# A hybrid backbone in one program: the held expert tile as 64 tokens by two slots, summed by TensorE alone

## The chip, the cores and the metric

One core of a Trainium2 chip runs the whole program once. The metric is the device time in microseconds (us), as the median of several executions. Engines: PE is TensorE, DVE VectorE, ACT ScalarE, POOL GpSimd, SP the engine that issues most plain transfers.

## What is computed

Two layers over 512 latent and 256 context tokens of width 1024. A layer is a modulated RMS norm, one input projection whose columns feed a gated delta rule, a Fourier branch and a convolution branch, an output projection, and then PEER, a retrieval of single-neuron experts. PEER is what the change touches:

```python
def blk(args):                 # 128 tokens; 128 experts for each of them
    hb, eb, gb = args
    act = jax.nn.gelu(jnp.einsum("tkd,td->tk", u_tab[eb], hb))
    return jnp.einsum("tk,tkd->td", gb * act, v_tab[eb])
```

For each token, 128 rows of 8 KB (a U row and a V row of 1024 floats) are gathered; each U row gives a dot product with the token's vector h, its gelu times the gate weight gives a coefficient, and the V rows are summed with these coefficients. The sum goes into the residual stream through a gate.

## The kernel before

All is f32. A tile is 128 tokens, a slot is the k-th of the 128 experts of every token of a tile. One slot is one indirect DMA from POOL that gathers 128 rows of 8 KB (1.05 MB), one dot product on DVE (L347, L2606), three small steps on ACT (gelu, gate weight, and the coefficients on the diagonal of a 128x128 matrix), and two matmuls on PE, diagonal by V row half, that add into two PSUM banks.

The function peer does the tiles of layer 0, six of them, but leaves out the last one (context tokens 128 to 255). That held tile is done by class HeldTile inside projection_latents, the stage in which layer 1's input projection of the latent tokens is computed, so that gathers run beside matmuls. The stage in order:

- SP loads four pieces of h (L759), three of 18 weight chunks, waits for the last row's store, and goes on with the chunks as PE uses them up (L766).
- PE does 18 chunks of 8 matmuls of 512 columns (L779); after k = 0, 2, 3, 5, 6, 7 it calls held.pe for one slot. In chunks 7 to 14 an 8-column matmul (L791) sums squares. Then come four row blocks, of 8 times two matmuls of 264 columns (L801, L803), with five slots each. PE does its queue in order: a slot whose diagonal isn't ready stops the products behind it.
- ACT calls held.act for six slots a chunk, then copies the chunk's product out of PSUM (L820), and from chunk 6 on does a silu (L824) and to chunk 13 a square (L830) of an earlier chunk. Silu and gelu need different tables (ACT_TABLE_LOAD). In a row block it does five slots and three copies (L855 to L857).
- DVE does the dots, and between them the taps of the two convolutions.
- POOL gathers into a ring of six buffers (HELD_RING); before gather g it waits until slot g - 6 is used up.

The held tile's slots are shared between two engines. on_dve says which: in chunks 6 to 17 every third slot, elsewhere two of three. A slot on DVE is added by one scalar_tensor_tensor (L369) to yacc, one on PE by diagonal (L386) and two matmuls (L397) to PSUM banks 1 and 3. That gives 67 slots to PE and 61 to DVE. The next stage, branches_beside_context, adds the two sums (L1101).

The first six gathers of the held tile are issued at the end of peer, on POOL, behind the last tile's gathers and a wait for the tile's expert numbers (eid_ready). In peer, SP's queue is a loop over the tiles; its last turn (i = M) waits for x_ready, which DVE signals when the last tile's sum is in the residual, and stores the row (L2556). A stage ends with a barrier of all engines behind the last instruction of each.

## Time and profile before

| | us |
|---|---|
| median of 3 runs (4364.39 to 4365.87) | 4364.73 |
| the profiled execution, whole | 4367.23 |
| its span | 4365.4 |
| PE busy in the span | 3693.1 |
| DVE busy | 3006.0 |
| ACT busy | 1720.2 |
| POOL busy | 1645.7 |
| the held stage, start to start of the next | 2310.6 to 2690.6 |

"Busy" is the time in which an engine executes something; PE's ends are modelled, so start-to-start times are the safer reading for it. PEclk is the clock that TensorE was granted, as a share of full speed. The DMA share is the mean busy share of 16 DMA engines. In brackets behind a timeline row stands the idle time before it and what ended it. "x4" on a PE row is four instructions; an f32 matmul is two of them. A shape such as 128*64 is rows by columns of the weights.

### The profile page before, as it was taken

What the parts mean: (1) busy time and instruction counts of PE and PEld (TensorE: products, weight loads), DVE (VectorE), ACT (ScalarE), POOL (GpSimd) and SP (SyncE); (2) the same over time, 40 slices, a digit from 0 to 9 for tenths busy, and PEclk for the clock granted to TensorE, in tenths of its full rate; (3) what the DMA queues carried; (4) which work ended last, traced back from release to release, by engine and by line L of the source; (5) the groups of instructions that cost most, each with busy time, mean ns of one, the idle gap of its engine ahead of it and who ended that gap; (6) DMA issues with size and microseconds to landing.
All of it is one profiled execution on the core that took longest, in us unless ns stands there. A gap on an engine that the chain in (4) does not pass through costs nothing. (4 is left out here: it accounts for less than half of the span.)

```text
span 4365.4 us, 55131 instructions
## 1 busy us (share of the span) xinstructions
PE 3693.1 (85%) x18945; PEld 1903.6 (44%) x18945; DVE 3006.0 (69%) x6251; ACT 1720.2 (39%) x5270; POOL 1645.7 (38%) x1508
## 2 busy tenths in 40 slices
PE   7998998988888887888886888888898888888777
PEld 3566854533433433433432335775443343343222
DVE  3964666975775875875875885557797687687444
ACT  2223623444344344344342454353444433433333
POOL 0004513443443443444443432352444444444332
PEclk9999999999999999999998999899999999999999
DMA  8360159999999999999999997015999999999997
GB/s 336 122 239 29 37 198 367 416 421 421 418 415 422 414 417 421 407 420 422 410 412 369 408 394 303 2 37 190 404 422 421 421 421 421 421 413 421 422 421 325
DMA packets 238985, 1506.07 MB, mean 345 GB/s; under 512 B 28433, under 2 KB 33617, under 8 KB 71153
## 3 DMA queue, kind: packets, MB, share of 16 engines
q0 software_dynamic: 184320, 1342.26, 74.7%
q1 hardware_dynamic: 54384, 160.28, 9.9%
q8 instruction: 150, 2.46, 0.2%
q14 instruction: 131, 1.07, 0.1%
HBM read 1490.32 MB, written 12.12 MB: 344 GB/s over the span
## 5 line engine op out<-in xcount | busy, mean ns | idle before, releaser
L2831 PE MATMUL ps<-low,pediag 128*128 128x512 f32 x2180 | 1058.7, 615 | 226.1 <-ACT pediag L2741 219.3
L2606 DVE CUSTOM_DVE_ANT_0 low<-low,hc 128x1024 f32<-128x1024 f32 x545 | 667.8, 1225 | 359.3 <-DMA low<-in_experts_dram,eid 342.0
L2585 POOL DMA_INDIRECT low<-in_experts_dram,eid x539 | 595.0, 1104 | 812.4 <-PE ps L2831 783.2
L2733 ACT ACTIVATE low<-peact 128x1 f32<-128x1 f32 x1152 | 232.1, 201 | 1335.0 <-DVE peact L2606 1334.0
L2831 PEld LDWEIGHTS ps<-low,pediag 128*128 128x128 f32 x2180 | 388.9, 192 | 824.5 <-ACT pediag L2741 499.4
L2741 ACT ACTIVATE pediag<-cst,low 128x128 f32<-128x128 f32 x1152 | 462.5, 402 | 42.1 <-PE ps L2831 4.5
L2831 PE MATMUL ps<-wide_a,pediag 128*128 128x512 f32 x640 | 307.8, 612 | 54.4 <-ACT pediag L2741 54.2
L2736 ACT ACTIVATE low<-low,gw 128x1 f32<-128x1 f32 x1152 | 339.1, 294 | 37.4
L2831 PE MATMUL ps<-wide_b,pediag 128*128 128x512 f32 x640 | 303.3, 605 | 50.7 <-ACT pediag L2741 48.5
L2060 PEld LDWEIGHTS ps<-qkvT,arena 128*128 128x128 f32 x2560 | 312.0, 193 | 75.4 <-issue 75.4
L2060 PE MATMUL ps<-qkvT,arena 128*128 128x128 f32 x2560 | 313.1, 276 | 2.4 <-ACT qkvT L2024 2.4
L2606 DVE CUSTOM_DVE_ANT_0 wide_a<-wide_a,hc 128x1024 f32<-128x1024 f32 x160 | 196.2, 1226 | 97.3 <-DMA wide_a<-in_experts_dram,eid 91.2
L2606 DVE CUSTOM_DVE_ANT_0 wide_b<-wide_b,hc 128x1024 f32<-128x1024 f32 x160 | 196.2, 1226 | 96.9 <-DMA wide_b<-in_experts_dram,eid 91.4
L2585 POOL DMA_INDIRECT wide_a<-in_experts_dram,eid x158 | 169.8, 1074 | 237.4 <-PE ps L2831 232.7
L2831 PE MATMUL ps<-last_b,pediag 128*128 128x512 f32 x456 | 219.4, 608 | 46.2 <-ACT pediag L2741 44.9
L2831 PE MATMUL ps<-last_a,pediag 128*128 128x512 f32 x456 | 220.5, 612 | 43.0 <-ACT pediag L2741 41.6
L2585 POOL DMA_INDIRECT wide_b<-in_experts_dram,eid x158 | 176.2, 1115 | 195.8 <-PE ps L2831 188.5
L2831 PEld LDWEIGHTS ps<-wide_a,pediag 128*128 128x128 f32 x640 | 114.4, 193 | 227.1 <-ACT pediag L2741 134.8
L2831 PEld LDWEIGHTS ps<-wide_b,pediag 128*128 128x128 f32 x640 | 113.5, 189 | 217.5 <-ACT pediag L2741 120.5
L2606 DVE CUSTOM_DVE_ANT_0 low<-last_b,hc 128x1024 f32<-128x1024 f32 x114 | 139.7, 1225 | 80.9 <-DMA last_b<-in_experts_dram,eid 77.6
L2606 DVE CUSTOM_DVE_ANT_0 low<-last_a,hc 128x1024 f32<-128x1024 f32 x114 | 139.6, 1225 | 76.1 <-DMA last_a<-in_experts_dram,eid 72.2
L2585 POOL DMA_INDIRECT last_b<-in_experts_dram,eid x112 | 121.4, 1084 | 163.1 <-PE ps L2831 156.0
(497 smaller groups left out, 5773.9 us busy)
## 6 DMA issues: line engine op xcount, KB each, us to landing
pjdot<-in_mod_t_dram SPq DMA_DIRECT2D x64, 512.0 KB, 5.2
arena<-in_w_mod_dram SPq DMA_DIRECT2D x24, 1024.0 KB, 14.4
arena<-in_peer_wq_dram SPq DMA_DIRECT2D x8, 2048.0 KB, 17.1
low<-in_experts_dram,eid POOLq DMA_INDIRECT x609, 8.7
pjw<-in_w_cols_dram SPq DMA_DIRECT2D x18, 512.0 KB, 3.7
plw<-in_w_cols_dram SPq DMA_DIRECT2D x18, 512.0 KB, 8.1
x_rows<-low SPq DMA_DIRECT2D x10, 512.0 KB, 7.7
qkvT<-mod_rows SPq DMA_DIRECT2D x9, 512.0 KB, 7.6
```

The costliest lines, as they stand in the source:

```text
L2060: last = self.nc.tensor.matmul(self.kit.ps[:, 4 + q % 2, 0:P], self.kit.wq[:, i, q * P:(q + 1) * P], self.hT[:, i, :], start=i == 0, stop= ...
L2585: nc.gpsimd.indirect_dma_start(ring.row(g), None, table, bass.IndirectOffsetOnAxis(eid[:, j % 2, k:k + 1], 0)).then_inc(ring.landed(g), 16)
L2606: nc.vector.tensor_tensor_reduce(out=dot_out if final else ring.row(g)[:, 0:D], in0=ring.row(g)[:, 0:D], in1=hc[:, j % 2, :], scale=1.0, s ...
L2733: nc.scalar.activation(ge[:, g % 2, 0:1], act_v[:, j % 2, k:k + 1], ACT.Gelu_apprx_tanh).then_inc(gelu_ready, 1)
L2736: nc.scalar.activation(ge[:, g % 2, 1:2], ge[:, g % 2, 0:1], ACT.Copy, scale=gw[:, j % 2, k:k + 1]).then_inc(weighed, 1)
L2741: nc.scalar.activation(diag[:, g % DIAGS, :], ident, ACT.Copy, scale=ge[:, g % 2, 1:2]).then_inc(diag_ready, 1)
L2831: last = nc.tensor.matmul(ps[:, half, :], diag[:, g % DIAGS, :], ring.row(g)[:, D + half * 512:D + (half + 1) * 512], start=k == 0, stop=k ...
```

## The change

What it does:

- The held tile is laid out anew: gather g brings 64 tokens' rows for two slots (partitions 0 to 63 the one, 64 to 127 the other); gathers 0 to 63 are for tokens 0 to 63, the others for tokens 64 to 127. For this the expert numbers, the gate weights and h are copied between partitions by small DMAs (spread, spread_rows).
- All 128 slots are summed on PE: the weights are a 128x64 matrix, two diagonals one above the other, so a matmul sums the two slots. The V row's left half goes to PSUM partitions 0 to 63, the right half to 64 to 127. A ring of four such matrices replaces three of 128x128. The adds on DVE and yacc go.
- The next stage gates the four quarters out of PSUM; two of them are moved to their partitions first, by two copies and two matmuls.
- The h pieces and the first three weight chunks are loaded by peer's SP code, behind its loop, into room that the query weights leave. The expert numbers' copies stand between the two. POOL waits for them (eid_in) ahead of the first held gather.
- A matrix of ones leaves the constants.

```diff
+HELD_DIAGS = 4
 HELD_A_CHUNK = 6
 HELD_A_ROW = 5
-HELD_SEMS = ["dotted", "gelu_ready", "weighed", "diag_ready", "summed", "added", "row_saved"]
+HELD_SEMS = ["dotted", "gelu_ready", "weighed", "diag_ready", "summed", "row_saved", "h_in", "w_in", "eid_in", "gw_in",
+             "rows_in"]
...
-        TAPS_FROM, TAPS_TO = 6 * HELD_A_CHUNK, 18 * HELD_A_CHUNK
-        spare = lambda g: g % 3 == 1 if TAPS_FROM <= g < TAPS_TO else g % 3 != 0
-        self.on_dve = [spare(g) for g in range(SLOTS)]
-        self.n_dve = [sum(self.on_dve[:g]) for g in range(SLOTS + 1)]
-        self.n_pe = [g - self.n_dve[g] for g in range(SLOTS + 1)]
-        self.issued = self.dots = self.adds = self.scaled = self.sums = 0
-
-    def work_in(self, parts, yacc):
-
-        self.yacc = yacc
-        self.act_v, self.ge, self.coef = (parts[:, i * SLOTS:(i + 1) * SLOTS] for i in range(3))
-        self.diag = parts[:, 3 * SLOTS:(3 + HELD_DIAGS) * SLOTS].rearrange("p (a n) -> p a n", n=P)
-
-    def free(self, eng, g):
-
-        if self.on_dve[g]:
-            eng.wait_ge(self.added, self.n_dve[g + 1])
-        else:
-            eng.wait_ge(self.summed, self.n_pe[g + 1])
+        self.issued = self.dots = self.scaled = self.sums = 0
+
+    def work_in(self, parts):
+
+        self.act_v, self.ge, self.coef, self.gw = (parts[:, i * SLOTS:(i + 1) * SLOTS] for i in range(4))
+        self.diag = parts[:, 4 * SLOTS:4 * SLOTS + HELD_DIAGS * 64].rearrange("p (a n) -> p a n", n=64)
+
+    def spread(self, sp, out, src, sem):
+
+        for half in range(2):
+            for part in range(2):
+                sp.dma_start(out[part * 64:(part + 1) * 64, half * 64:(half + 1) * 64],
+                             src[half * 64:(half + 1) * 64, part * 64:(part + 1) * 64]).then_inc(sem, 16)
+
+    def spread_rows(self, sp):
+
+        h = self.kit.hc
+        for part in range(2):
+            sp.dma_start(h[part * 64:(part + 1) * 64, 0, :], h[0:64, 1, :]).then_inc(self.rows_in, 16)
+        sp.wait_ge(self.rows_in, 32)
+        sp.dma_start(h[0:64, 1, :], h[64:128, 1, :]).then_inc(self.rows_in, 16)
 
     def gathers(self, pool, upto):
 
         for g in range(self.issued, min(upto, SLOTS)):
             if g >= HELD_RING:
-                self.free(pool, g - HELD_RING)
+                pool.wait_ge(self.summed, g - HELD_RING + 1)
             self.gather(g)
...
-            bass.IndirectOffsetOnAxis(self.eid[:, g:g + 1], 0)).then_inc(self.e_in[g % HELD_RING], 16)
+            bass.IndirectOffsetOnAxis(self.kit.eid2[:, g:g + 1], 0)).then_inc(self.e_in[g % HELD_RING], 16)
...
     def dve(self, dve, n):
 
         for g in range(self.dots, self.dots + n):
+            if g % 64 == 0:
+                dve.wait_ge(self.rows_in, 32 + 16 * (g // 64))
             row = self.rows[g % HELD_RING][:, 0:D]
             dve.wait_ge(self.e_in[g % HELD_RING], 16 * (g // HELD_RING + 1))
-            self.nc.vector.tensor_tensor_reduce(out=row, in0=row, in1=self.h, scale=1.0, scalar=0.0, op0=ALU.mult,
-                                                op1=ALU.add, accum_out=self.act_v[:, g:g + 1]).then_inc(self.dotted, 1)
-            if g >= 2:
-                self.add(dve, g - 2)
+            self.nc.vector.tensor_tensor_reduce(out=row, in0=row, in1=self.kit.hc[:, g // 64, :], scale=1.0, scalar=0.0,
+                                                op0=ALU.mult, op1=ALU.add, accum_out=self.act_v[:, g:g + 1]
+                                                ).then_inc(self.dotted, 1)
         self.dots += n
...
-    def add(self, dve, g):
-
-        if not self.on_dve[g] or g < self.adds:
-            return
-        self.adds = g + 1
-        row, coef = self.rows[g % HELD_RING][:, D:2 * D], self.coef[:, g:g + 1]
-        dve.wait_ge(self.weighed, g + 1)
-        if self.n_dve[g] == 0:
-            self.nc.vector.tensor_scalar(self.yacc, row, coef, None, ALU.mult).then_inc(self.added, 1)
-        else:
-            dve.wait_ge(self.added, self.n_dve[g])
-            self.nc.vector.scalar_tensor_tensor(out=self.yacc, in0=row, scalar=coef, in1=self.yacc,
-                                                op0=ALU.mult, op1=ALU.add).then_inc(self.added, 1)
-
...
     def act(self, act, n):
 
         for g in range(self.scaled, self.scaled + n):
+            if g == 0:
+                act.wait_ge(self.gw_in, 64)
             act.wait_ge(self.dotted, g + 1)
             self.nc.scalar.activation(self.ge[:, g:g + 1], self.act_v[:, g:g + 1], ACT.Gelu_apprx_tanh
                                       ).then_inc(self.gelu_ready, 1)
             act.wait_ge(self.gelu_ready, g + 1)
             self.nc.scalar.activation(self.coef[:, g:g + 1], self.ge[:, g:g + 1], ACT.Copy,
                                       scale=self.gw[:, g:g + 1]).then_inc(self.weighed, 1)
-            if not self.on_dve[g]:
-                i = self.n_pe[g]
-                act.wait_ge(self.weighed, g + 1)
-                if i >= HELD_DIAGS:
-                    act.wait_ge(self.summed, i - HELD_DIAGS + 1)
-                self.nc.scalar.activation(self.diag[:, i % HELD_DIAGS, :], self.kit.c("ident"), ACT.Copy,
-                                          scale=self.coef[:, g:g + 1]).then_inc(self.diag_ready, 1)
+            act.wait_ge(self.weighed, g + 1)
+            if g >= HELD_DIAGS:
+                act.wait_ge(self.summed, g - HELD_DIAGS + 1)
+            self.nc.scalar.activation(self.diag[:, g % HELD_DIAGS, :], self.kit.packed("I")[:, 0, :], ACT.Copy,
+                                      scale=self.coef[:, g:g + 1]).then_inc(self.diag_ready, 1)
         self.scaled += n
 
     def pe(self, pe, n):
 
         for g in range(self.sums, self.sums + n):
-            if not self.on_dve[g]:
-                i = self.n_pe[g]
-                pe.wait_ge(self.diag_ready, i + 1)
-                for half, b in enumerate(self.BANKS):
-                    last = self.nc.tensor.matmul(self.kit.ps[:, b, :], self.diag[:, i % HELD_DIAGS, :],
-                                                 self.rows[g % HELD_RING][:, D + half * 512:D + (half + 1) * 512],
-                                                 start=i == 0, stop=i == self.n_pe[SLOTS] - 1)
-                last.then_inc(self.summed, 1)
+            pe.wait_ge(self.diag_ready, g + 1)
+            for half in range(2):
+                last = self.nc.tensor.matmul(self.kit.ps[half * 64:(half + 1) * 64, self.BANKS[g // 64], :],
+                                             self.diag[:, g % HELD_DIAGS, :],
+                                             self.rows[g % HELD_RING][:, D + half * 512:D + (half + 1) * 512],
+                                             start=g % 64 == 0, stop=g % 64 == 63)
+            last.then_inc(self.summed, 1)
         self.sums += n
...
-                for t in range(NL):
-                    sp.dma_start(hT[:, :, t * P:(t + 1) * P], h_d[t].rearrange("p (k n) -> p k n", k=KD)
-                                 ).then_inc(h_in, 16)
+                held.spread_rows(sp)
+                held.spread(sp, held.gw, kit.gw[:, held.j % 2, :], held.gw_in)
+                sp.wait_ge(held.row_saved, 16)
                 for c, off in enumerate(chunks):
-                    if c == RING:
-                        sp.wait_ge(held.row_saved, 16)
-                    if c >= RING:
+                    if c < RING:
+                        continue
+                    if c >= 2 * RING:
                         sp.wait_ge(proj_ready, c - RING + 1)
                     sp.dma_start(w[:, c % RING, :, :], w_chunk(kit, L, off)).then_inc(w_in[c % RING], 16)
...
-                pe.wait_ge(h_in, 16 * NL)
+                pe.wait_ge(held.h_in, 16 * NL)
+                pe.wait_ge(held.w_in, 16 * RING)
                 for c in range(NF):
-                    pe.wait_ge(w_in[c % RING], 16 * (c // RING + 1))
+                    w_now = w[:, c % RING] if c >= RING else held.w[:, c]
+                    if c >= RING:
+                        pe.wait_ge(w_in[c % RING], 16 * (c // RING))
                     if c >= 2:
                         pe.wait_ge(proj_read, c - 1)
...
+                pe.wait_ge(far_read, 2)
+                for at, rows in ((lo, hi), (hi, lo)):
+                    last = nc.tensor.matmul(ps[at, 7, :], ident[:, rows], far[:], start=True, stop=True)
+                last.then_inc(far_moved, 1)
...
-                for c in range(2):
-                    last = nc.vector.tensor_tensor(two(moved)[:, c, :], two(yacc)[:, c, :], ps[:, 1 + 2 * c, :], ALU.add)
-                link(last)
+                nc.vector.tensor_copy(far[hi, :], ps[hi, 1, :]).then_inc(far_read, 1)
+                nc.vector.tensor_copy(far[lo, :], ps[lo, 3, :]).then_inc(far_read, 1)
                 for c in range(2):
                     dve.wait_ge(mean_ready, c + 1)
                     nc.vector.tensor_tensor(acc[:, c, :], acc[:, c, :], ps[:, 2 * c, :], ALU.subtract
                                             ).then_inc(cent_ready, 1)
                 dve.wait_ge(gate_in, 16)
-                link(nc.vector.tensor_tensor(moved, moved, gate_c, ALU.mult))
+                left, right = slice(0, 512), slice(512, D)
+                for rows, cols, bank in ((lo, left, 1), (hi, right, 3), (lo, right, 7), (hi, left, 7)):
+                    if bank == 7:
+                        dve.wait_ge(far_moved, 1)
+                    last = nc.vector.tensor_tensor(moved[rows, cols], ps[rows, bank, :], gate_c[rows, cols], ALU.mult)
+                link(last)
...
                 sp.wait_ge(x_saved, 16 * (M - 1 if held else M))
+                if held:
+                    sp.wait_ge(sc.q_ready, HP * (N - 1) + LATE)
+                    for t in range(NT - NC):
+                        sp.dma_start(held.hT[:, :, t * P:(t + 1) * P], kit.h_d[t].rearrange("p (k n) -> p k n", k=KD)
+                                     ).then_inc(held.h_in, 16)
+                    sp.wait_ge(sc.eid_ready, late_numbers + N - 1)
+                    held.spread(sp, kit.eid2, eid[:, (N - 1) % 2, :], held.eid_in)
+                    for c in range(PL_RING):
+                        sp.dma_start(held.w[:, c], w_chunk(kit, L + 1, latent_chunks()[c])).then_inc(held.w_in, 16)
...
                 if held:
-                    pool.wait_ge(sc.eid_ready, late_numbers + N - 1)
+                    pool.wait_ge(held.eid_in, 64)
                     pool.wait_ge(sc.q_ready, HP * (N - 1) + LATE)
```

## Rows read from the trace of the kernel before

**Rows 1.** Windows: us, busy of PE, PEld, DVE, ACT, POOL, PEclk, DMA share, GB/s

```profile
2328.80:2461.00 132.20, 101.25 (x203) 40.83 (x201) 94.73 (x129) 40.48 (x117) 57.97 (x46) 0.92 0.97 391
...
2461.00:2633.00 172.00, 153.48 (x337) 61.40 (x338) 150.77 (x221) 86.76 (x209) 64.96 (x60) 0.98 0.99 393
...
2633.00:2690.60 57.60, 48.06 (x168) 32.17 (x166) 41.12 (x55) 29.97 (x72) 20.87 (x16) 0.94 0.85 325
```

**Rows 2.** Timeline (start us, us, engine): ScalarE's copies of chunks 0, 7, 12, 17

```profile
2339.22 0.60 ACT L820 ACTIVATE arena<-ps 128x512 f32<-128x512 f32 x1 [18.48 <-PE ps L779]
...
2461.01 0.58 ACT L820 ACTIVATE arena<-ps 128x512 f32<-128x512 f32 x1
...
2547.96 0.60 ACT L820 ACTIVATE arena<-ps 128x512 f32<-128x512 f32 x1 [0.84 <-PE ps L779]
...
2632.98 0.60 ACT L820 ACTIVATE arena<-ps 128x512 f32<-128x512 f32 x1 [3.56 <-PE ps L779]
```

**Rows 3.** Timeline, ScalarE's path from chunk 11's copy to the next slot on PE

```profile
2530.91 0.60 ACT L820 ACTIVATE arena<-ps 128x512 f32<-128x512 f32 x1 [1.16 <-PE ps L779]
...
2534.13 1.28 ACT L376 ACT_TABLE_LOAD   x1
...
2535.98 0.40 ACT L386 ACTIVATE parts<-cst,parts 128x128 f32<-128x128 f32 x1
...
2536.44 1.98 PE L397 MATMUL ps<-arena,parts 128*128 128x512 f32 x4 [1.90 <-ACT parts L386]
```

**Rows 4.** Timeline of PE: products, a slot, an 8-column sum, a product

```profile
2511.88 1.88 PE L779 MATMUL ps<-wide_a,plw 128*128 128x512 f32 x4
2513.59 1.88 PE L397 MATMUL ps<-low,parts 128*128 128x512 f32 x4
2515.40 1.02 PE L791 MATMUL ps<-arena 128*8 128x512 f32 x2
2516.36 1.12 PE L779 MATMUL ps<-wide_a,plw 128*128 128x512 f32 x2
```

**Rows 5.** Timeline of PE in the scan: 64-column weights, alternate halves, 128 columns

```profile
2953.96 1.09 PE L1846 MATMUL ps<-scS,arena 128*64 128x128 f32 x16
2954.88 1.04 PE L1855 MATMUL ps<-scS,qkvT 128*64 128x128 f32 x16
```

**Rows 6.** Timeline at the change from the last tile to the held stage

```profile
2302.51 0.94 POOL L333 DMA_INDIRECT low<-in_experts_dram,eid  x1 [0.30 <-issue]
...
2309.47 0.32 SPq L2556 DMA_DIRECT2D x_rows<-qkvT  x1
...
2310.84 9.32 SPq L759 DMA_DIRECT2D wide_a<-h_turned  x4
...
2326.94 2.04 PE L779 MATMUL ps<-wide_a,plw 128*128 128x512 f32 x2 [20.02 <-DMA plw<-in_w_cols_dram]
...
2328.78 2.68 PE L397 MATMUL ps<-arena,parts 128*128 128x512 f32 x4
```

**Rows 7.** Waits in the held stage: total us, times, longest

```profile
POOL low L333 <- DVE low L369: 67.4, 33, 4.7
```

**Rows 8.** Timeline of ScalarE in the row blocks and at their end

```profile
2650.61 0.39 ACT L855 ACTIVATE low<-ps 128x264 f32<-128x264 f32 x1 [4.09 <-PE ps L803]
...
2652.65 0.20 ACT L376 ACTIVATE parts<-parts 128x1 f32<-128x1 f32 x1
...
2688.77 0.39 ACT L855 ACTIVATE low<-ps 128x264 f32<-128x264 f32 x1 [0.32 <-PE ps L803]
```

**Rows 9.** DMA issues of whole span, then both stage changes: median landing last

```profile
pjw<-in_w_cols_dram SPq DMA_DIRECT2D x18, 512.0 KB, 3.7
...
wide_a<-h_turned SPq DMA_DIRECT2D x4, 512.0 KB, 8.3
...
cialog<-in_a_log_dram SPq DMA_DIRECT2D x1, 4.0 KB, 10.4
```

**Rows 10.** Timeline of VectorE in the stage after

```profile
2707.24 1.23 DVE L1112 SCALAR_TENSOR_TENSOR arena<-arena 128x1024 f32<-128x1024 f32 x1 [7.95 <-DMA arena<-mod_rows]
```

More of the change, by code:

```diff
@@ L35 @@
 NEG = -3.0e38
-CONSTS = (["ident", "L0", "L1", "M0", "M1", "CH0", "CH1", "ones", "gmean", "C64", "S64"]
+CONSTS = (["ident", "L0", "L1", "M0", "M1", "CH0", "CH1", "gmean", "C64", "S64"]
           )
@@ L717, in _, with latent_chunks, projection_latents @@
                 nc.gpsimd.memset(row_eps[0:H, :], EPS * P).then_inc(padded, 1)
-def projection_latents(nc, kit, L, h_d, hT, qkvT, zs, ab, fT, acc, held):
+def latent_chunks():
+    return ([C_OFF + c * P for c in range(4)] + [c * P for c in range(NQKV)] + [F_OFF + c * P for c in range(2)])
+def projection_latents(nc, kit, L, room, qkvT, zs, ab, fT, acc, held):
     NCV, NFN = 4, 2
-    chunks = ([C_OFF + c * P for c in range(NCV)] + [c * P for c in range(NQKV)]
-              + [F_OFF + c * P for c in range(NFN)])
+    chunks = latent_chunks()
     ROWS = SEQ // GRID_W
     W = GRID_W + 2 * HALO
-    RING = 3
+    RING = PL_RING
     NF = len(chunks)
@@ L744, in projection_latents @@
         ZH = ZA // 2
-        two = lambda at: kit.arena[:, at:at + 2 * SEQ].rearrange("p (c n) -> p c n", c=2)
+        hT = held.hT
+        two = lambda i: room[:, i * 2 * SEQ:(i + 1) * 2 * SEQ].rearrange("p (c n) -> p c n", c=2)
         wz = kit.arena[:, 0:KD * ZA].rearrange("p (k n) -> p k n", k=KD)
-        at = KD * ZA
-        aT, gT, pT, yT = (two(at + i * 2 * SEQ) for i in range(4))
-        sq, root = aT, kit.arena[:, at + 2 * SEQ:at + 3 * SEQ]
+        aT, gT, pT, yT = (two(i) for i in range(4))
+        sq, root = aT, room[:, 2 * SEQ:3 * SEQ]
         at = PL_SPREAD
@@ L778, in _ @@
                     for k in range(KD):
-                        last = nc.tensor.matmul(ps[:, b, :], w[:, c % RING, k, :], hT[:, k, :],
+                        last = nc.tensor.matmul(ps[:, b, :], w_now[:, k, :], hT[:, k, :],
                                                 start=k == 0, stop=k == KD - 1)
@@ L910, in _ @@
                 held.dve(dve, NL * HELD_A_ROW)
-                held.settle(dve)
                 dve.wait_ge(root_turned, 1)
@@ L992, in branches_beside_context @@
         csq = sb("csq", [P, 2, SEQ])
+        far = sb("far", [P, 512])
+        lo, hi = slice(0, 64), slice(64, P)
         hT = sb("hT", [P, KD, CTX])
@@ L2979, in constants @@
          "M1": same & (i < j), "CH0": (i < CHUNK) & (j >= 0), "CH1": (i >= CHUNK) & (j >= 0),
-         "ones": np.ones((P, P)), "gmean": (i // 64 == j // 64) / 64.0}
+         "gmean": (i // 64 == j // 64) / 64.0}
     ang = 2 * np.pi * ((i % 64) * (j % 64) % 64) / 64
```

37 lines of the change are left out of this document (18 added, 19 removed).

## The prediction

> **What bounds the kernel now.** I read the windows of the held stage first: what each engine and the DMA did in its three parts [rows 1]. The stage runs from 2310.6 to 2690.6 us. In the middle part, 2461 to 2633, the DMA share reads 0.99 at 393 GB/s, which looks like a DMA bound, while PE is busy for 153.5 of 172 us and VectorE for 150.8. So the shares don't settle it, and I went to the order of events. ScalarE's copies of the chunks' products (L820) mark the 18 chunks [rows 2]: chunk 0 at 2339.22, chunk 7 at 2461.01, chunk 12 at 2547.96, chunk 17 at 2632.98. From chunk 11 [rows 3] to chunk 12 it is 17.05 us, and six of the ten steps from chunk 7 on are 17.04 to 17.06. So even a period is that of a fixed chain, not of transfers.
>
> The chain is readable in one chunk [rows 3]. The last product of chunk 11 lets ScalarE copy at 2530.91; it then loads a table, does a silu and a square, loads the table back (2534.13) and builds the next slot's diagonal, which ends at 2536.38; PE, 1.90 us idle, starts that slot at 2536.44. From copy to slot is 5.53 us, and nothing of it is the slots' cost. A chunk then has 7 more product matmuls and, on PE, slots. A 512-column f32 matmul is two MATMUL instructions: four take 2513.59 - 2511.88 = 1.71 us [rows 4], so an instruction is 0.43, a matmul 0.855, a slot's pair 1.71. In the period stand 7 x 0.855 = 5.98 and three of the four PE slots of these chunks (the fourth follows the last product and lies beside ScalarE's path): 5.98 + 3 x 1.71 + 5.53 = 16.64, and 0.4 for the way from the last product to the copy and for changes of mode gives the 17.05. PE and ScalarE in turn set this part. VectorE and GpSimd aren't on it, though GpSimd waits long for VectorE's adds [rows 7]: the next gathers already stand behind it, and DVE isn't what PE waits for.
>
> **The change, part by part.** The profiled execution took 4367.23 us (span 4365.4), the median is 4364.73; I add differences in us to the profiled one and carry the sum to the median, 2.5 lower.
>
> *VectorE's adds go.* The 61 adds of the code leave. In the period above they lie beside PE, so I cost that at nothing from chunk 7 on. The seven steps before that take 121.8 us [rows 2], 17.4 each, with VectorE's padding and first convolutions at their end. I take 16.2 for six of them (PE's own time is 6.84 + 6 x 1.48 = 15.7, see below) and 19 for the last, 116 in all: -5.8. The bounds are 0 (nothing was due to the adds) and -9 (15.7 for the six).
>
> *Every slot goes to PE.* Per chunk six slots instead of two (chunks 0 to 5) or four, per row block five instead of one or two. All depends on what one slot, two calls with 64 columns of weights each, costs between full matmuls; call it S. No row has such a pair with 512 columns between full ones. The nearest is the scan, which writes alternate halves of the partitions with 64-column weights, in the same order of calls: 16 instructions of 128 columns take 2954.88 - 2953.96 = 0.92 us [rows 5]. By the rate of [rows 4], 0.107 for 128 columns, they would take 1.71 in a row. So the two halves do overlap, 2.15 units of time for four instructions. The calls come as A1 A2 B1 B2. Taken in order, A2 must wait for A1 (same columns), B1 starts beside A2, B2 beside the next A1. In a stream this gives 2 units a pair, as seen. A lone pair between full matmuls has nothing beside A1 and B2: 3 units, 1.28. Between full and narrow there is a price: slot to the 8-column sum 1.81 where 1.71 is the work, and that sum to the next full matmul 0.96 where 0.86 is: 0.10 at each change [rows 4]. So S = 1.28 + 0.19 = 1.48. Bounds: 0.86 (full overlap, no change price) and 1.90 (none, with it).
>
> The Trainium skill's "TensorE: Matmul & The Clock Gate", section "Part 3: Packing small matmuls", says that matmuls in distinct column groups run concurrently with starts about 4 ns apart, and "TensorEngine Tiling (Array Packing)", section "Key Properties", that a change of tiling mode drains the array. The trace agrees with both where it can: 0.92 for 1.71, and 0.10 a change. By the first alone a lone pair would be 2 units; rival 1 below works this out from the rows. The same section says that matmuls start and end in program order, and this gives my 3 units, since the halves of one f32 call come first.
>
> Now the sums. Chunk 0: from slot 0 to the copy, 5.98 + 5 S + 0.2 = 13.6, before 10.4 (2328.78 to 2339.22): +3.1. From chunk 7 on the period is 5.98 + 5 S + 5.95 = 19.3 (the 5.95 is 17.05 less the 5.98 and 5.13 above, so it carries all that I can't itemize). The square, 0.65, is missing from the last three: 7 x 19.3 + 3 x 18.65 = 191.1, before 171.97: +19.1. Row blocks: ScalarE copies the first at 2650.61, the last at 2688.77 [rows 8]. After a copy the first gelu is 2.04 us off [rows 8], the first diagonal by three steps of some 0.3 to 0.4 later 3.5; six of the eight steps of two 264-column matmuls, 264/512 of 1.71 = 0.88 each, and four slots stand in the cycle: 3.5 + 4 S + 6 x 0.88 = 14.7, thrice, and 1 for the turned roots (an estimate), 45.2 against 38.2: +7.0. From chunk 17 to the first, 17.6 now, with three more slots of which the longer ScalarE path hides most: +1.5. Together 3.1 - 5.8 + 19.1 + 1.5 + 7.0 = +24.9. The slope is 71 slots, so 71 us for each us of S.
>
> *The first loads, and the way into the stage.* The diff puts them behind SP's loop. SP's queue there first waits for the last row's x_ready, so they can't start before the store at 2309.47 [rows 6]: they are ahead of the stage's start by 1.4 us only. In that queue come four h loads (now issued 2310.84 to 2320.16, 9.3 us), then the four pieces of the expert numbers, then three weight loads. Behind the numbers' semaphore stands GpSimd with the held tile's first six gathers, the last of which it issues at 2302.51 now; and behind GpSimd the barrier that ends the phase, so all engines. Count: h issued 2309.9 to 2317 (less traffic beside them), the numbers land behind them at about 2323 (h landings 8.3 us in the median [rows 9]), six gathers at 0.94 + 0.30 end at 2331, the barrier as now 1.1: the stage starts at about 2332 and not at 2310.6. In it SP must first copy h to both halves and then the gates' weights: two copies, wait, one copy, four small ones. A loaded queue lands a 4 KB load only after 10.4 us [rows 9], the shortest landing on the page is 3.7 us, for 512 KB [rows 9]. The queue empties meanwhile, so I take 4 for the copies and 5 for the small ones, 2 for issuing: 11, then three ScalarE steps 1.0. PE has k 0 of chunk 0 behind it and waits in order for slot 0, at about 2344 by this count. Now it is at 2328.78, after 20.02 us of waiting for weights, which go. So +15 (bounds +8 with short landings, +22 with loaded ones). The stretch from 2302 to 2323 has no gather in the DMA queues; since PE and ScalarE set the later pace, only the start is lost.
>
> *After the stage.* The far halves cost two copies, two narrow matmuls and four quarter products in place of two adds and one product, some +2 us on VectorE, to be ready by 2698. The next thing VectorE waits for lands at 2707.24, after 7.95 us of idleness [rows 10]: nothing. If that cover were gone it would be +2. The smaller constants (no "ones") cost nothing.
>
> **Sum:** +15 + 24.9 = +39.9: profiled 4407.1, median **4405**.
>
> **Rivals.**
> 1. *Full overlap.* A and B run side by side in a lone pair too: 2 units, S = 0.86 + 0.19 = 1.05. For it: the scan's stream doesn't tell 2 units from 3 for a lone pair. Against: A2 stands before B1 in the queue. -0.43 x 71 = -30.4: +9.5, 4374.
> 2. *No overlap, S = 1.90* (512 columns from two places of SBUF are more than the scan's 128). Against: the scan's four are from two places too. +0.42 x 71 = +30, and chunks 1 to 7 become bound by PE (6.84 + 6 x 1.9 = 18.2 each, +14): +84, 4449.
> 3. *Not slower: the pairs are free of the change.* Full overlap and no price for changing the mode, S = 0.86, so 71 x 0.62 = -44, with the short start of +8: 8 + 24.9 - 44 = -11, 4354. It decides from S = 0.91 at a start of +15, or 1.01 at +8; above that it isn't faster. For it: VectorE's 61 adds are truly gone, and GpSimd waits 67.4 us for adds of one tile alone [rows 7]. Against: the 0.10 at each change.
> 4. *The start isn't delayed* (the numbers land early, the barrier overlaps): 0 instead of +15, 4390. Against: SP's order. This is also the case that the change does what its words say, loads a tile ahead; in the diff they aren't.
>
> **How the numbers follow.** Forecast 0.55, rival 1 0.17, rival 2 0.07, rival 3 0.11, rival 4 0.10. A measurement of this kernel can tell about 0.2%, 8.7 us, so 4356 to 4373.5 is no change. Rival 3 gives faster 0.09 and same 0.02; rival 1, at the edge, same 0.09 and slower 0.08; the rest slower: 0.09, 0.11, 0.80. The range leaves out rival 3 and most of rival 2: from rival 1's 4373 to 4428, which is the forecast with the long start and S = 1.7.
>
> **What would show it.** In the profile after: GpSimd's first L333-like gather after 2320 instead of at 2288.6; the stage's first memset at about 2332; slot 0 on PE at 2342 to 2350; a period between chunk copies of 19.3 in place of 17.05, PE idle for some 2 us once in it, and DMA share in the middle down from 0.99 to about 0.88; a lone pair at 1.28 from start to start of its neighbours less 0.2. Wrong it would be if the period stays at 17 (rival 1, then all of the loss is the start), if it is 21.4 (rival 2), or if six gathers are issued before the last row's store.

## The result

The changed kernel takes 4394.6 us (median; 4391.3 to 4398.0), the kernel before 4365.3 in the same job: a ratio of 1.0058, 95% interval 1.0046 to 1.0071, so 29 us slower. The forecast was 4405, "slower". Its direction holds and its size is 10 us too large; below, the terms turn out to be off in both directions. Three slow executions of the runs below (14001 us of e7_order_act, 8453 and 6166 us of e10_h_late_both) are left out of their ratios.

The profiled execution took 4397.01 us, span 4395.0 against 4365.4. First the windows of the kernel after; columns are us, then the busy time of PE, PEld, DVE, ACT, POOL, then PEclk, DMA share, GB/s:

```profile
2300.00:2310.00 10.00, 6.61 (x14) 2.03 (x12) 4.45 (x8) 2.69 (x9) 0.00 (x0) 1.00 0.03 11
2310.00:2324.00 14.00, 0.00 (x0) 0.00 (x0) 0.57 (x1) 0.00 (x0) 1.36 (x2) 0.55 0.95 269
...
2349.20:2475.60 126.40, 113.26 (x314) 29.73 (x314) 64.90 (x104) 51.37 (x157) 55.04 (x47) 0.99 0.99 404
2475.60:2659.70 184.10, 158.89 (x418) 40.60 (x420) 128.92 (x204) 90.20 (x228) 67.52 (x60) 0.94 0.96 370
2659.70:2721.00 61.30, 56.33 (x220) 28.28 (x220) 22.47 (x37) 33.37 (x85) 18.53 (x16) 0.97 0.78 293
```

Against [rows 1], chunks 7 to 17 (second line from below) grew from 172 to 184 us, at fewer GB/s and at a lower PEclk. And from 2300 to 2310 us the DMA engines move next to nothing, where in the kernel before they are full:

```profile
2300.00:2310.00 10.00, 5.92 (x12) 2.00 (x12) 4.91 (x6) 1.79 (x6) 1.97 (x2) 0.99 1.01 421
```

ScalarE's copies of the products of chunks 0, 7 and 17 are the marks, as in [rows 2] (timeline: start us, us, engine):

```profile
2362.85 0.60 ACT L812 ACTIVATE wide_a<-ps 128x512 f32<-128x512 f32 x1 [7.69 <-PE ps L771]
...
2475.59 0.58 ACT L812 ACTIVATE wide_a<-ps 128x512 f32<-128x512 f32 x1
...
2659.71 0.60 ACT L812 ACTIVATE arena<-ps 128x512 f32<-128x512 f32 x1 [6.39 <-PE ps L771]
```

The row blocks' first copy is at 2678.33 and the last at 2719.03 (2650.61 and 2688.77 before, [rows 8]). The last row store of the tile before is 1.1 later than in [rows 6], slot 0 stands at 2349.24. So the sum can be made term by term:

| term, us | forecast | measured |
|---|---|---|
| row store to slot 0 | +15 | 38.64 - 19.31 = +19.3 |
| slot 0 to copy 0 | +3.1 | 13.61 - 10.44 = +3.2 |
| copy 0 to copy 7 | -5.8 | 112.7 - 121.8 = -9.1 |
| copy 7 to copy 17 | +19.1 | 184.1 - 172.0 = +12.2 |
| copy 17 to first row | +1.5 | 18.6 - 17.6 = +1.0 |
| rows | +7.0 | 40.7 - 38.2 = +2.5 |
| sum | +39.9 | +29.1 |

With the tile before (+1.1) that is 30.2 at the last row copy; the spans differ by 29.6.

**The start** in the kernel after, timeline:

```profile
2310.60 0.32 SPq L2559 DMA_DIRECT2D x_rows<-qkvT  x1
2311.03 4.85 SPq L2580 DMA_DIRECT2D arena<-h_turned  x4
2315.92 3.49 SPq L317 DMA_DIRECT2D eid<-eid  x4
2319.45 1.53 SPq L2585 DMA_DIRECT2D arena<-in_w_cols_dram  x3
2322.34 0.94 POOL L337 DMA_INDIRECT arena<-in_experts_dram,eid  x1 [32.89 <-DMA eid<-eid]
...
2325.28 1.17 SPq L324 DMA_DIRECT2D hc<-hc  x2
...
2328.55 0.94 POOL L337 DMA_INDIRECT low<-in_experts_dram,eid  x1 [0.30 <-issue]
2329.49 1.37 POOL L908 MEMSET arena<- 128x1504 f32 x1
...
2337.84 1.23 DVE L353 CUSTOM_DVE_ANT_0 arena<-arena,hc 128x1024 f32<-128x1024 f32 x1 [27.27 <-DMA hc<-hc]
2338.33 2.52 SPq L317 DMA_DIRECT2D parts<-gw  x4
...
2348.28 0.20 ACT L364 ACTIVATE parts<-parts 128x1 f32<-128x1 f32 x1 [42.27 <-DMA parts<-gw]
...
2349.24 1.12 PE L381 MATMUL ps<-arena,parts 128*64 128x512 f32 x2 [20.65 <-ACT parts L372]
```

Read it as a chain: store, expert numbers, first gather (2322.34; 2288.6 before), h copied to both halves (issued 2325.28, landed 2337.84), gate weights (issued from 2338.33, landed 2348.28), slot 0. The engines enter the stage while GpSimd still issues the six gathers (SP's copy at 2325.28, the last gather at 2328.55): the barrier did not stand behind them, as the forecast had it.

**A lone slot** between products, and PE over a short stretch just behind the slot's start:

```profile
2539.82 0.59 PE L771 MATMUL ps<-arena,plw 128*128 128x512 f32 x1
2540.34 1.08 PE L381 MATMUL ps<-low,parts 128*64 128x512 f32 x4
2541.35 1.13 PE L771 MATMUL ps<-arena,plw 128*128 128x512 f32 x2
2542.40 1.08 PE L381 MATMUL ps<-low,parts 128*64 128x512 f32 x4
```

```profile
2540.34 0.65 PE L381 MATMUL ps<-low,parts 128*64 128x512 f32 x2
```

The second view is of 2540.42 to 2540.46 only: two of the slot's four instructions have begun, though one unit of 0.43 isn't over yet; the other two follow half a microsecond behind the first two. The two column halves run side by side, so the work is two units of 0.43. From the slot to the product behind it is 1.01 where 0.86 is the work, from that product to the next slot 1.05 where 0.855 is the product: 0.15 and 0.19 more, 0.35 for both changes together. S = 0.86 + 0.35 = 1.21, between the forecast's 1.48 and rival 1's 1.05.

**A chunk in the stretch from 7 to 17**: the windows of chunks 9 and 10, then PE at the start of chunk 10:

```profile
2494.90:2512.60 17.70, 15.14 (x44) 3.84 (x44) 14.15 (x24) 9.17 (x23) 6.49 (x7) 1.00 0.99 385
2512.60:2531.90 19.30, 16.75 (x44) 4.19 (x44) 13.95 (x23) 9.17 (x23) 6.56 (x7) 0.91 0.93 359
```

```profile
2514.41 1.12 PE L771 MATMUL ps<-arena,plw 128*128 128x512 f32 x2
2518.09 1.08 PE L381 MATMUL ps<-arena,parts 128*64 128x512 f32 x4 [2.55 <-ACT parts L372]
2519.09 3.35 PE L771 MATMUL ps<-arena,plw 128*128 128x512 f32 x4
```

PE's wait for ScalarE at each chunk's start, 1.90 us in [rows 3], is 2.55 now. After it, in five of the ten chunks, the clock falls to its lower level, 1.2 GHz, for a moment: four instructions take 3.35 us where they else take 1.98, and PEclk of the chunk reads 0.91. Three such chunks take 19.3 us against 17.7 of a clean one. The last two of the ten have no square and would take 17.0, as the one before them does:

```profile
2604.30:2621.30 17.00, 15.11 (x44) 3.81 (x44) 12.42 (x20) 8.64 (x22) 8.50 (x7) 1.00 0.97 387
2621.30:2641.20 19.90, 17.05 (x42) 4.41 (x44) 11.52 (x20) 8.65 (x23) 7.60 (x7) 0.83 0.89 328
2641.20:2659.70 18.50, 15.71 (x42) 4.17 (x44) 8.63 (x14) 8.55 (x22) 6.03 (x7) 0.91 0.96 340
```

How many chunks are met is partly chance: with the same wait of 2.55, two of the ten read a lower clock in e1_early below, five in e2_early_all and four in e6_order.

### The profile page after: what moved, and what is told of

Its sections match the earlier page's. It is cut to its first block and busy times, and to the rows that moved or that the text cites. A ratio compares the mean times of both kernels' runs of the same rounds, so it can differ in the third digit from the quotient of the medians.

```text
span 4395.0 us, 55644 instructions
## 1 busy us (share of the span) xinstructions
PE 3713.8 (84%) x19193; PEld 1864.7 (42%) x19193; DVE 2937.1 (67%) x6193; ACT 1735.2 (39%) x5331; POOL 1646.6 (37%) x1508
## 5 line engine op out<-in xcount | busy, mean ns | idle before, releaser
L2843 PEld LDWEIGHTS ps<-wide_b,pediag 128*128 128x128 f32 x640 | 113.5, 189 | 220.9 <-ACT pediag L2753 127.3
L2597 POOL DMA_INDIRECT last_b<-in_experts_dram,eid x112 | 124.1, 1108 | 160.2 <-PE ps L2843 153.1
```

The costliest lines, as they stand in the source:

```text
L2597: nc.gpsimd.indirect_dma_start(ring.row(g), None, table, bass.IndirectOffsetOnAxis(eid[:, j % 2, k:k + 1], 0)).then_inc(ring.landed(g), 16)
L2843: last = nc.tensor.matmul(ps[:, half, :], diag[:, g % DIAGS, :], ring.row(g)[:, D + half * 512:D + (half + 1) * 512], start=k == 0, stop=k ...
```

## The experiments

The theory after reading the two traces: (1) the lost start is SP's chain of small copies; (2) a slot's halves overlap, and S is set by them and the price of the mode change; (3) from chunk 7 on PE and ScalarE in turn set the time, and the longer wait with its clock drops is what was lost. The rivals: the bytes that the DMA engines must move set the start, and the pace as well. Twelve kernels were run; ratios are to the kernel before in the same job.

### Nothing side by side: e3_same_half

```diff
-                last = matmul(ps[half * 64:(half + 1) * 64, BANKS[g // 64], :], ..., start=g % 64 == 0, stop=g % 64 == 63)
+                last = matmul(ps[0:64, BANKS[g // 64], :], ..., start=g % 64 == 0 and half == 0,
+                              stop=g % 64 == 63 and half == 1)
```

> The kernel after, with both products of a slot on the same column half of the array (left and right halves of the V rows are summed in one place, so the part of the output that the held tile gives is not what the reference asks). Nothing can then lie side by side. Theory (the halves run in pairs, A1 with B1 and A2 with B2): a slot's pair takes four units of 0.43 in place of two, so its cost goes from 1.21 to about 2.06 us and the period of a chunk with six slots from 17.7 by 4 x 0.85 for the lone slots and 0.85 or so for the two adjacent ones to 22; over 18 chunks and 4 rows some 75 us more than after, unless the weight loads hide better: 4450 to 4475 us. Rival (no overlap of halves in the kernel after): 4395, the same.

One execution: 4475.2 us, span 4473.1, 78 more than after. A slot and its successor on PE:

```profile
2533.81 1.93 PE L381 MATMUL ps<-low,parts 128*64 128x512 f32 x4
2535.68 1.12 PE L772 MATMUL ps<-arena,plw 128*128 128x512 f32 x2
```

From slot to product it is 1.87 in place of 1.01, two units more, and the period of chunks 7 to 17 is 21.9. By 71 slots the 0.86 would be 61, but with S = 2.07 chunks 0 to 7 are bound by PE as well (137.4 us between copies 0 and 7), as rival 2 had it. So the halves overlap fully, even in a lone slot.

### The loads really a tile ahead: e1_early, e2_early_all, e6_order

```diff
                 for i in range(M + 1):
+                    if held and i == M:
+                        sp.wait_ge(sc.q_ready, HP * (N - 1) + LATE)
+                        ... the four h loads, the respread of eid, the three weight loads
                     if i >= 1:
                         sp.wait_ge(x_ready, i)
```

> The kernel after, with one edit: the first loads of the stage and the respread of the expert numbers are queued on SP before it waits for the last tile's rows, not behind their store; the gate weights and rows of h are still copied in the stage. Theory (the lost start is a chain of waits on SP): the six held gathers leave at about 2290 us and land before the stage starts, slot 0 then waits for the copies of h and of the gate weights alone, landed some 10 + 10 us after the stage's start at about 2312, so slot 0 stands near 2333 where it stood at 2349.2: 16 us less, about 4379 us. Rival (the DMA engines' bytes set the start): 2298 to 2310 us, in which the engines moved next to nothing, hold about 4 MB, so at most 10 us come back, about 4385. Rival (the start is not what costs): 4394.

Measured: 1.0033 (1.0020 to 1.0045), 4384.5 us. By the ratios it is 11 us less than after, but the two intervals nearly touch, so the time alone can't tell the bytes rival's 10 from the 16. Slot 0 stands at 2341.15, 8 us earlier than in the kernel after and not 16.

e2_early_all adds the copies of h (tokens 0 to 63, doubled, into free columns of arena) and of the gate weights to the early block, so that only one copy is left in the stage.

> As the kernel with early loads, and the gate weights and the doubled rows of h are copied in the stage before too (h for the first 64 slots into a free place of arena). No copy is left in the stage but the one for slots 64 to 127. Theory: slot 0 waits for its dot product and the three ACT instructions alone and stands near 2316 us, 33 us before the 2349.2 of the kernel after: about 4362 us, even with the kernel before (4365). Rival (bytes): 4 MB of loads and copies and 6 MB of gathers need 25 us of the DMA engines from about 2290 on, so the slots of the first chunks wait for their rows instead and only 15 to 20 us come back: 4375 to 4380.

Measured: 1.0019 (1.0010 to 1.0029), 4377.4 us: 17 less than after. Slot 0 stood at 2333.3, not at 2316. SP's queue in e1_early shows one reason:

```profile
2270.10 35.54 SPq L2560 DMA_DIRECT2D arena<-h_turned  x4
2305.68 5.05 SPq L317 DMA_DIRECT2D eid<-eid  x4
2310.78 1.53 SPq L2565 DMA_DIRECT2D arena<-in_w_cols_dram  x3
```

The four h loads take SP 35.5 us to issue here, against 4.85 in the kernel after; everything queued behind them is late. e6_order puts them last in the early block.

> As the kernel with all loads and copies early, but SP queues them in another order behind the last tile's expert numbers: the expert numbers, the rows of h, the gate weights, the three weight chunks, and the 2 MB of turned h last. Theory (in the run before, the loads of h, queued first in small pieces while the engines were full, held up SP for 36 us and so everything behind them): the expert numbers are spread at about 2290 us, the held gathers leave at once and fill the idle 2298 to 2310 us, and slot 0 stands at 2317 to 2320 us in place of 2333.3: about 4363 us. Rival (bytes set it, whatever the order): slot 0 moves by 5 us at most, 4372 or more.

Measured: 1.0023 (1.0013 to 1.0032), 4377.8 us: no gain on e2_early_all. The order worked as meant and didn't help:

```profile
2283.32 2.48 SPq L319 DMA_DIRECT2D eid<-eid  x4
...
2291.26 36.20 SPq L2570 DMA_DIRECT2D arena<-h_turned  x4
2327.50 1.43 SPq L2575 DMA_DIRECT2D x_rows<-qkvT  x1
...
2332.70 2.07 PE L775 MATMUL ps<-arena 128*128 128x512 f32 x2 [20.05 <-DMA arena<-h_turned]
```

```profile
2300.00:2310.00 10.00, 7.19 (x12) 2.72 (x12) 4.38 (x8) 3.02 (x11) 2.08 (x3) 0.83 1.01 414
2310.00:2332.00 22.00, 1.99 (x4) 0.68 (x4) 4.30 (x5) 1.06 (x4) 1.59 (x6) 0.62 0.95 339
```

The gap from 2300 to 2310 is full again (414 GB/s for 11), the share from there to PE's start is 0.95, and PE waits for h. The start of the kernel after had 10 idle us of the DMA engines in it and two landings in series; take both away and slot 0 still stands at 2333 to 2335 (2336.8 in e9_h_late_act below), most likely by the engines' own work. Of the 20 us lost, 15 come back.

### The same for the kernel before: e4_before_early

The diff of e1_early, without the expert numbers (no respread there), on the kernel before and its own sums.

> The kernel before with its own held tile (128 tokens a slot, sums on DVE and TensorE), and only the first loads of the next stage (h and three weight chunks) queued on SP before its wait for the last tile's rows. Theory (the start is a chain of waits): PE begins at about 2313 us in place of 2328.8, 15 us less: about 4350 us. Rival (bytes): the DMA engines are full to 2310 us in the kernel before and moved 293 GB/s from 2310 to 2328.8 against 420 before, so 5 us at most come back: about 4360 us. Rival (nothing comes back, the bytes of the loads delay the last tile's gathers by as much): 4365.

Measured: 1.0001 (0.9992 to 1.0011). Slot 0 stood at 2333.8 in place of 2328.8, and the row store at 2323.5 in place of 2309.5: the last rival. The engines were full up to 2310 us anyway, so what is loaded ahead delays the tile that is still running.

### Two edits of the slots' order: e7_order_act, e8_order_pairs

```diff
-                    held.act(act, HELD_A_CHUNK)
+                    held.act(act, HELD_A_CHUNK * (c + 1) - held.scaled)
 ...
                         evacuate(c, fT[:, n - NQKV, :], ACT.Copy)
+                    if c + 1 < NF:
+                        held.act(act, 1)
                     n = c - LAG
```

> As e6_order, and ACT makes the first diagonal of the next chunk between copying this chunk's product out and its silu and square, so that TensorE's wait at each chunk's start (2.55 us in the kernel after) falls away. Theory (this wait, and the clock drop that follows it in four of ten chunks, is what a chunk has lost besides the slots' cost): the period of chunks 7 to 17 falls from 18.4 on average to about 16.8, 16 us less over ten chunks: 4347 us if e6_order gives 4363. Rival (the DMA engines set that stretch: 6.8 MB a chunk at 421 GB/s take 16.2 us, and the gathers' turnaround more): 17.5, 9 us less.

Measured: 0.9975 (0.9965 to 0.9986). Copy 7 to copy 17 took 161.5 us, where e6_order had 182.4. With this edit the new layout beats the kernel before.

```diff
-                        if k not in (1, 4):
-                            held.pe(pe, 1)
+                        if k in (1, 4, 7):
+                            held.pe(pe, 2)
```

> As e6_order, and the six slots of a chunk stand two and two behind products 1, 4 and 7 instead of singly behind 0, 2, 3, 5, 6 and 7 (the products of the rows as before). Theory (a change between 128-wide and 64-wide products costs 0.35 us both ways together): half of the changes go, 1.05 us less a chunk, and TensorE comes to the first slot one product later, which takes 0.86 from its wait for ACT: 1.9 us less a chunk where the DMA engines are not the bound (chunks 7 to 17), 15 to 19 us less than e6_order. Rival (the change costs nothing and the 1.21 of a slot is its products' own time): the pair of slots takes 2.4 us and only the 0.86 a chunk comes back, 8 us.

Measured: 0.9977 (0.9967 to 0.9987), 21 us less than e6_order, and copy 7 to copy 17 took 157.9. Copy 0 to copy 7, which the expectation had left out, took 118.3 us where e6_order had 113.3, so the pairs cost some 5 us there. A pair of slots without a wait between them, on PE:

```profile
2501.30 1.08 PE L386 MATMUL ps<-arena,parts 128*64 128x512 f32 x4 [1.36 <-ACT parts L377]
2502.21 1.03 PE L386 MATMUL ps<-low,parts 128*64 128x512 f32 x4
2503.17 2.84 PE L775 MATMUL ps<-arena,plw 128*128 128x512 f32 x6
```

The two together take 1.87 and not twice 1.01, and the wait for ScalarE is 1.36. So the change of mode has its price, but the two effects of this edit can't be told apart by its time. The windows say why both edits give the same. They are those of copy 7 to copy 17, first of e8_order_pairs, then of e12_after_act (below):

```profile
2465.30:2623.20 157.90, 142.67 (x420) 41.73 (x418) 125.19 (x198) 90.78 (x228) 75.35 (x60) 1.00 1.01 419
```

```profile
2476.00:2636.20 160.20, 149.67 (x418) 38.09 (x418) 126.07 (x201) 92.06 (x227) 67.36 (x60) 1.00 1.01 420
```

A chunk is 6 gathers of 1.05 MB and 0.52 MB of weights, 6.8 MB, 16.2 us at 420 GB/s. With a share of 1.00 to 1.01 that is the floor that stands behind the chain of PE and ScalarE, and either edit reaches it. (Six of the ten chunks of e9_h_late_act take 16.2. The ten together can come out a little under 162 us, since the last two move fewer bytes.)

### The ACT edit alone: e12_after_act on the kernel after, e5_before_act on the kernel before

> The kernel after, its start as it is, with the ACT edit alone: the first diagonal of the next chunk before this chunk's silu and square. Theory (the 2.55 us wait at each chunk's start and the clock drops behind it are on the path of the kernel after): period of chunks 7 to 17 at 16.2 to 16.5 us in place of 18.4 on average, which is 18 us less there and 2 less in the rows: 4375 us in place of 4394.6, so two thirds of what the change cost. Rival (the gain seen in the kernels with early loads came with their earlier start): period still 17.7 or more, 4390.

Measured: 1.0006 (0.9996 to 1.0015), 4372.6 us. Its start is that of the kernel after (slot 0 at 2348.84); copy 7 to copy 17 is 160.2 us against 184.1, its mean clock full (window above), and the waits of PE fell, as the theory had it:

```profile
2514.58 1.08 PE L381 MATMUL ps<-low,parts 128*64 128x512 f32 x4 [1.07 <-ACT parts L372]
```

So one slot a chunk, moved ahead on ScalarE, takes back 22 of the 29 us, with the start still slow.

> The kernel before, with one edit: ACT makes its first slot of the next chunk (and its diagonal) before this chunk's silu and square. Theory (TensorE's wait of 1.90 us at each chunk's start is on the path in chunks 7 to 17): the period falls from 17.05 toward the 16.2 us in which the DMA engines can move a chunk's 6.8 MB at 421 GB/s: 8 to 10 us less, about 4356 us. Rival (the wait only takes up slack that DVE's or the gathers' pace leaves): the same within 3 us.

Measured: 0.9988 (0.9978 to 0.9997): 5 us or so where 8 to 10 were expected; copy 7 to copy 17 takes 167.3 us against 172.0, at 402 GB/s. The kernel before has less to gain. Its DMA share in this stretch is 1.00 already: the engines are busy all the time and yet move 402 GB/s and not 420. Why, I did not settle.

### h behind the store: e9_h_late_act, e10_h_late_both, e11_before_w_act

e9_h_late_act is e7_order_act with the h loads back behind the row store, e10_h_late_both adds the pairs, e11_before_w_act is the kernel before with the ACT edit and the three weight chunks early.

> As e7_order_act (64-token slots, small copies and weights early, first diagonal of a chunk before silu), but the 2 MB of turned h are queued on SP behind the last tile's row store, as in the kernel after. Theory (h's small pieces, not its place in the order, were what slot 0 waited for: 36 us to issue in full engines in both early kernels, 5 us at the stage's start): the row store goes out near 2311 us again, h takes 5 to 9 us behind it and lands at about 2321, slot 0 stands at 2323 in place of 2334.4: 11 us less than e7_order_act, about 4348 us. Rival (bytes): 2 MB of h and the gathers need the engines as long as before, slot 0 at 2330 or later: 4354 or more.

Measured: 0.9982 (0.9973 to 0.9992). Slot 0 at 2336.8, the bytes rival's place: the row store went out at 2315.2, but the h loads then took SP 13 us, since the six gathers filled the engines, and PE waited for h until 2334.8.

> As e9_h_late_act, with the slots two and two behind products 1, 4 and 7. Theory (with either edit the engines already move 420 GB/s in chunks 7 to 17, a chunk in 16.2 us, and nothing is left to gain there): within 4 us of e9_h_late_act. Rival (both edits add, TensorE's time is still on the path): period 15.2, 10 us less.

Measured: 0.9985 (0.9975 to 0.9995), as e9_h_late_act: nothing left to add. Two of its ten chunks read a PEclk of 0.90, where e9_h_late_act has none.

> The kernel before with its own held tile (128 tokens a slot, sums on DVE and TensorE), the ACT edit, and the first three weight chunks early (h behind the row store, as before). Theory: TensorE's first product waits for h alone, at about 2321 us in place of 2327.3, so 4 to 6 us less than the kernel before with the ACT edit alone: about 4358 us against 4368 for the kernel before in this job. Against e9_h_late_act it shows what the 64-token slots are worth once their start is mended: about 8 us in chunks 0 to 7, where DVE has no adds, and 2 to 4 in chunks 7 to 17. Rival (slots of 64 tokens are worth nothing): e9_h_late_act and this kernel the same within 3 us.

Measured: 0.9989 (0.9980 to 0.9999), no better than e5_before_act. PE's first product was at 2331.1 and not at 2321. Between this and e9_h_late_act lies 0.0007, within the intervals: with both mended, what the 64-token slots are worth against the 128-token ones is about 0.1% and at most 0.2%, and these ratios can't tell it from nothing. In the chunks the gain is there, and larger than expected: 112.7 against 122.4 us from copy 0 to copy 7, 160.9 against 166.1 from copy 7 to copy 17. But of these 15 us some 11 go elsewhere: slot 0 stands 4 us later, the way from it to copy 0 is 3.5 longer, and from copy 17 to the last row copy it is 3.3 longer, where more slots stand on PE.

## Why the prediction was right in sign and off in size

*What bounds the kernel.* "PE and ScalarE in turn" was right: e12_after_act moves nothing but ScalarE's order and the stretch shrinks by 24 us. What the step lacked is the floor under it. From the 0.99 of the DMA share I concluded that the share doesn't settle the matter, and did not work out what a chunk costs in bytes: [rows 1] has 393 GB/s, and at the 420 that the engines reach in the better kernels 6.8 MB are 16.2 us, only 0.9 below the period of 17.05.

*The adds.* -9.1, at my outer bound; I had chosen -5.8, six steps of 16.2 and a last one of 19. The six took 91.4 together, the last 21.3. The DMA engines are full in a step of 15.0 (the fourth) and in the slow last one alike:

```profile
2406.50:2421.50 15.00, 14.16 (x42) 3.71 (x44) 6.31 (x12) 6.84 (x20) 7.12 (x7) 1.00 1.02 419
...
2454.30:2475.60 21.30, 14.38 (x40) 3.73 (x40) 13.37 (x21) 9.29 (x25) 6.15 (x6) 1.00 1.01 423
```

Seven chunks of 6.8 MB at 420 GB/s are 113.5 us, measured were 112.7, and a shorter path on ScalarE changes nothing (112.2 us in e7_order_act, 113.1 in e12_after_act). So it was most likely the engines' floor that ended this gain, and not PE's 15.7; no run moved fewer bytes to show it. The first step, 14.1, is PE's own time with the measured S: 6.84 + 6 x 1.21.

*S, the step that failed.* The count of three units rested on A2 standing before B1 in the queue. The Trainium skill's "TensorE: Matmul & The Clock Gate", section "Part 3: Packing small matmuls", says that matmuls begin and end in program order, and I drew from it that B1 can't begin until A2 has. The trace shows two of the four at 2540.34 together, and e3_same_half two units more without the overlap: two units, 0.86, rival 1's mechanism. In which order the four stand in the queue, the trace doesn't name; either it isn't the one that I assumed, or the rule doesn't hold for them. I also wrote that the scan's stream doesn't tell two units from three. It does, at its start. This view of the kernel before is of 2953.97 to 2954.00:

```profile
2953.96 0.33 PE L1846 MATMUL ps<-scS,arena 128*64 128x128 f32 x2
```

Two instructions have begun within 0.04 us, though a unit is 0.107 there. By my order the second would be A2, which has to wait for A1. Against this, the price of the change was sized too low: 0.35 both ways, not 0.19. The row that I took it from [rows 4] changes between 128 and 8 columns for one product only; between the 64-column pair and a product no row of before had it. A part was in that row all the same: the product behind the 8-column sum is 1.12 long, two instructions else 1.02, so 0.10 more of the price lies inside the product, where I didn't look. The two errors, -0.43 and +0.16, leave S at 1.21, and -0.27 x 71 = -19. (The terms written with S hold 5 + 50 + 12 = 67 slots, which gives -18; where the other four of my 71 stand, the prediction doesn't say.)

*The period.* With S = 1.21 my formula gives 5.98 + 5 x 1.21 + 5.95 = 17.98; clean chunks took 17.69. The ten took 184.1 because the wait grew to 2.55 and five chunks met the lower clock. That cost about 1.6 us in three of them, 2.9 and 1.5 in the last two, 9 in all, and I had no term for it, though the kernel before has two such chunks of ten too (2495.10 to 2513.85 and 2614.95 to 2632.98). The formula at S = 1.21 gives 7 x 17.98 + 3 x 17.33 = 177.9 or +6 for the stretch; less 3, since the clean chunks are 0.3 shorter than the formula, and with the 9 that is +12, as measured. That the stretch came out within 7 us of the forecast's +19.1 is in part luck: the smaller S took 13 off it, and the clock drops that I had no term for gave 9 back. e12_after_act shows that the wait and the drops go together: in its window PEclk is 1.00. That the longer wait brings more drops than the 1.90 of the kernel before is likely and not shown, since e1_early has its two as well.

*The start, +15 against +19.3.* The expert numbers' landing (2323 forecast, first gather 2322.34) and the gathers' end (2331, 2329.49) were right. The barrier was not: the stage starts at 2324 and not at 2332. This 8 us too many was more than made up by the two landings in series, which I had taken at 4 and 5 by the argument that the queue empties. It doesn't: the six gathers fill it. The issues of 2310 to 2350 us, median us to landing last:

```profile
hc<-hc SPq DMA_DIRECT2D x3, 256.0 KB, 9.5
...
eid<-eid SPq DMA_DIRECT2D x4, 16.0 KB, 3.6
parts<-gw SPq DMA_DIRECT2D x4, 16.0 KB, 8.2
```

The expert numbers' copies, of the same 16 KB, were issued ahead of the gathers, beside the loads of h, and landed after 3.6. I had the loaded value, 10.4, in [rows 9], and kept it for the bound only. And "only the start is lost" was said of the stretch without gathers; that is right for the kernel after, but e4_before_early, e6_order and e9_h_late_act show that the cure is bound by the same engines.

*The rows, +7.0 against +2.5.* Twelve of their slots between copies at 0.27 less are 3.2 of the 4.5.

*After the stage.* As forecast, the far halves' products end before the next thing that VectorE waits for, a load with 7.94 us of idleness before it where [rows 10] has 7.95. That load itself lands 1.8 us later behind the last row copy than before; at the end of the span nothing of it is left (30.2 at the last row copy, 29.6 in the spans).

*Rivals.* Rival 1 was right in its mechanism and would have been 4374 with the forecast's start; with the measured change price (0.16 x 71 = 11) and start (+4) it comes to 4389. Rival 4 was half right (the barrier), with no gain. That the diff doesn't load ahead of the tile, and that loading is delayed behind the last store, was right.

The best kernels, e7_order_act and e8_order_pairs, are 0.25% and 0.23% faster than the kernel before, which the change alone made 0.58% slower. Part of this the kernel before gets from the ACT edit too (0.12%, e5_before_act), and the intervals of the two overlap.

## What to carry to other kernels

Work out a stage's floor in bytes before any chain: it caps every gain and says which losses will be felt. When an edit lengthens an engine's wait by half a microsecond a period, look at TensorE's clock in each period, not only at the mean; and ask first which order of the helper engine's work makes the wait, since one moved instruction group was worth more here (22 us) than the change itself cost at its start (19). A load that is moved ahead into a stretch whose engines are full is paid for by the work that runs there.

## What was new of the hardware

- Two f32 products of 512 columns on opposite column halves, alone between 128-column ones, start together and take 0.86 us, on the same half one after the other 1.72 (slot to product 1.01 against 1.87).
- Changing from 128-column to 64-column weights and back costs 0.35 us for both changes; of two slots in a row the second starts 0.91 behind the first.
- Four loads of 512 KB in 512-byte pieces took 4.85 us of SP's queue in the kernel after, where the engines had been idle, 13 beside six gathers (e9_h_late_act), and 35 to 39 with the engines nearly full (35.5 in e1_early, 39.1 in e4_before_early).
- Copies of 16 KB from one on-chip buffer to another landed 8.2 us after issue behind the six gathers, and 3.6 ahead of them.
